# RWKV input stage of a two-layer transformer block: slab order, place of the convolution taps, convolution in four groups inside a slab, inverse begun inside the last input slab

## What is computed

```python
p = rms_norm(x, gain) @ w_in_first          # 2816 columns: 11 slabs of 256
# columns 0..1023: conformer convolution, the rest: RWKV inputs
h = u[..., :512] * sigmoid(u[..., 512:1024])        # "value" and "gate"
h = depthwise_conv(h, conv_w, 31 taps) + conv_b     # then layer_norm, silu
p = p + mu * (prev_token(p) - p)                     # token shift mix
r, k, v, w_lo, a_lo, g_lo = split(p)
w = exp(-exp(-0.5) * sigmoid(w0 + tanh(w_lo) @ w_up))
a = sigmoid(a0 + a_lo @ a_up);  g = sigmoid(g_lo) @ g_up
kk = normalise_per_head(k * k_k);  k = k * (1 + (a - 1) * k_a)
y = recurrence(r, w, k, v, kk, a)                    # S_t = S w - (S kk)(kk a) + v k
bonus = sum(r * k * r_k) * v
```

## Time and profile before

| | |
|---|---|
| median of 3 runs | 914.25 us |
| the profiled execution's own time | 913.55 us |
| its span, first to last instruction | 911.7 us |
| mean granted TensorE clock | 0.990 of full speed |
| TensorE matmul busy | 858.5 us (94%) |
| VectorE busy | 567.5 us (62%) |
| ScalarE busy | 440.0 us (48%) |
| chain that ended last: TensorE / VectorE / ScalarE | 79% / 12% / 4% |
| input stage, first slab's matmul to the level-1 `t_mm` products | 426.06 to 527.62 us |

### The profile page before, as it was taken

One profiled execution on the slowest core, in us unless ns is written; L12 is line 12 of the kernel. 1 busy time (PEld: TensorE's weight loads), 2 busy tenths in 40 slices (PEclk: granted clock), 3 DMA queues, 4 the chain that ended last, 5 costly groups with the idle time before them and its releaser, 6 DMA issues.

```text
span 911.7 us, 18606 instructions
## 1 busy us (share of the span) xinstructions
PE 858.5 (94%) x7952; PEld 797.7 (87%) x7952; DVE 567.5 (62%) x671; ACT 440.0 (48%) x558; POOL 20.8 (2%) x31
## 2 busy tenths in 40 slices
PE   4999999998999999998988989999899799999997
PEld 4899999987999998888986889888897799999885
DVE  4475467476777776647599886566554655555444
ACT  4555755445555556436472401445544544444333
POOL 1110000000000002000000000000000000000000
PEclk9999999999999999999999999999999799999999
DMA  9853433556455555455433121144524355555541
GB/s 346 287 183 115 173 139 139 186 208 220 160 176 180 184 179 191 179 185 202 168 125 110 48 96 50 48 155 160 171 95 141 112 185 184 184 184 184 185 139 46
DMA packets 22253, 145.86 MB, mean 160 GB/s; under 512 B 2618, under 2 KB 2810, under 8 KB 6064
## 3 DMA queue, kind: packets, MB, share of 16 engines
q1 hardware_dynamic: 19008, 134.23, 42.2%
q0 software_dynamic: 2896, 10.13, 3.4%
q10 hardware_dynamic: 288, 0.59, 0.2%
HBM read 143.87 MB, written 1.07 MB: 159 GB/s over the span
## 4 chain that ended last, share of the span: by engine, by line
PE 79%; DVE 12%; ACT 4%; issue 3%; DMA 1%; DVEq 0%; ACTq 0%
PE ps L1629 23%; PE ps L1631 22%; PE ps L1630 22%; DVE w_lo L935 4%; ACT w_hi L470 2%; PE ps L2025 2%; PE ps L1973 1%; PE ps L1657 1%; DVE cacc L1293 1%; DMA norm_gain<-in_rows_vec 1%; DVE xn L1525 1%; PE ps L2190 1%; PE ps L2206 1%; DVE xn L989 1%; DVE x L1531 1%
## 5 line engine op out<-in xcount | busy, mean ns | idle before, releaser
L935 DVE TENSOR_TENSOR w_lo<-raw,w_hi 128x2048 fp32r<-128x2048 f32 x124 | 284.8, 2297 | 189.2 <-ACT w_hi L470 189.2
L1629 PE MATMUL ps<-hT_hi,w_hi 128*128 128x256 f32 x1240 | 356.2, 287 | 13.2 <-DVE hT_lo L996 7.1
L1630 PE MATMUL ps<-hT_lo,w_hi 128*128 128x256 f32 x1240 | 352.9, 285 | 0.0
L1631 PE MATMUL ps<-hT_hi,w_lo 128*128 128x256 f32 x1240 | 352.9, 285 | 0.0
L470 ACT ACTIVATE w_hi<-raw 128x2048 fp32r<-128x2048 f32 x125 | 239.1, 1912 | 174.6 <-PE ps L1631 174.1
L1629 PEld LDWEIGHTS ps<-hT_hi,w_hi 128*128 128x128 f32 x1240 | 240.2, 194 | 19.0 <-issue 16.1
L1630 PEld LDWEIGHTS ps<-hT_lo,w_hi 128*128 128x128 f32 x1240 | 240.1, 194 | 0.1
L1631 PEld LDWEIGHTS ps<-hT_hi,w_lo 128*128 128x128 f32 x1240 | 240.1, 194 | 0.0
L1629 PE MATMUL ps<-w_hi,gT_hi 128*128 128x512 f32 x176 | 69.8, 397 | 0.6 <-DVE w_lo L935 0.6
L1631 PE MATMUL ps<-w_hi,gT_lo 128*128 128x512 f32 x176 | 69.0, 392 | 0.0
L1630 PE MATMUL ps<-w_lo,gT_hi 128*128 128x512 f32 x176 | 68.4, 388 | 0.0
(11 more groups left out here) (286 smaller groups left out, 1043.2 us busy)
## 6 DMA issues: line engine op xcount, KB each, us to landing
raw<-in_weights SPq DMA_DIRECT2D x126, 1024.0 KB, 4.9
row_gain<-in_rows_vec POOLq DMA_DIRECT2D x4, 512.0 KB, 4.8
norm_gain<-in_rows_vec POOLq DMA_DIRECT2D x4, 512.0 KB, 4.7
bias<-bias_scratch POOLq DMA_DIRECT2D x1, 1536.0 KB, 9.5
x<-in_x SPq DMA_DIRECT2D x2, 512.0 KB, 5.2
xn<-in_mem POOLq DMA_DIRECT2D x2, 512.0 KB, 5.8
out<-x SPq DMA_DIRECT2D x4, 256.0 KB, 2.1
masks<-in_masks POOLq DMA_DIRECT2D x1, 768.0 KB, 12.4
```

The costliest lines, as they stand in the source:

```text
L935: V.tensor_tensor(w_lo[:, n % SPLIT, :], raw[:, n % RAW, :], w_hi[:, n % SPLIT, :].bitcast(F32), ALU.subtract).then_inc(sems["lo_ready"], 1)
L1629: mm(dst, left[0], right[0], start=first, stop=False)
L1630: mm(dst, left[0], right[1], start=False, stop=False)
L1631: return mm(dst, left[1], right[0], start=False, stop=last)
```

## The change

It does five things, all in the stage `in2` and the levels behind it.

1. The order of the input slabs: gate half 1, value half 1, lora, k, k, gate half 0, value half 0, r, r, v, v. The lora products move from behind slab 2 to behind slab 4, and their first eight, of 64 rows each, are issued alternately from the two halves of the array's rows. `spread` does the same with four products of 64 rows in place of 128.
2. In each turn of the loop ScalarE and VectorE do `splits(n0+i+2)` first and the token shift or gate after it; VectorE's taps now stand ahead of that split (`TAPS_FIRST`), some behind (`TAPS_AFTER`), three inside turn 7.
3. The product k * k_k moves from VectorE to ScalarE (4 instructions, signal `kk_ready`). The product r * k * r_k is split: ScalarE scales k (4 instructions, `k_weighted`), VectorE multiplies by r in one instruction, in level 2; r * P goes to level 2 too. `feat_ready` no longer waits for r.
4. TensorE does the convolution as four groups of 64, 60, 64 and 60 products inside slab 8, one behind each fourth step, and `spread` behind step 7.
5. `pair_products(0)` stands ahead of slab 10, the turned products behind its step 5, the products with the identity behind its step 9.

Nothing is changed in SyncE's and GpSimd's lists; SyncE loads the same 11 slabs, of which three stand in another order.

```diff
-IN2 = {"lora": 0, "gate": (5, 1), "value": (6, 2), "k": (3, 4), "r": (7, 8), "v": (9, 10)}
+IN2 = {"lora": 2, "gate": (5, 0), "value": (6, 1), "k": (3, 4), "r": (7, 8), "v": (9, 10)}
...
             for i in range(11):
+                if i < 10:
+                    splits(n0 + i + 2)
                 if i in IN2["gate"]:
...
-                splits(n0 + i + 2)
-                if i == 1:
-                    wait_unit(u0)
+                if i == 3:
+                    wait_unit(u0 + IN2["lora"])
...
                 elif i == 5:
-                    act.wait_ge(sems["kk_ready"], 1)
+                    wait_unit(u0 + IN2["k"][1])
+                    for t in range(4):
+                        A(rt("kk", t), rt("k", t), ACT.Copy, scale=vec[:, VEC["k_k"] + t:VEC["k_k"] + t + 1])\
+                            .then_inc(sems["kk_ready"], 1)
+                    act.wait_ge(sems["kk_ready"], 4)
...
-                elif i == 7:
+                elif i == 8:
                     conv_out()
-                elif i == 8:
+                    act.wait_ge(sems["feat_ready"], 1)
+                    for t in range(4):
+                        A(rt("k", t), rt("k", t), ACT.Copy, scale=vec[:, VEC["r_k"] + t:VEC["r_k"] + t + 1])                            .then_inc(sems["k_weighted"], 1)
+                elif i == 9:
                     conv_total()
+            splits(n0 + 12)
...
-            TAP_PLAN = {2: 4, 3: 5, 4: 2, 5: 5, 6: 6, 7: 8, 8: 1}
+            TAPS_FIRST = {2: 2, 3: 2, 4: 3, 5: 3, 6: 2, 7: 2, 8: 2}
+            TAPS_AFTER = {1: 2, 7: 5, 8: 5}
             mixed = [0]
             for i in range(11):
+                conv_taps(TAPS_FIRST.get(i, 0))
+                if i == 7:
+                    dve.wait_ge(sems["kkrs_ready"], 1)
+                    V.reciprocal(rs[:, :], rs[:, :]).then_inc(sems["kkinv_ready"], 1)
+                splits(min(n0 + i + 2, FIRST_SLAB["mem_b"] - 1))
...
+                    settle()
+                    do(V.tensor_tensor(rwide("Pinv"), rwide("k"), rwide("Pinv"), ALU.mult))
+                    conv_taps(3)
                     dve.wait_ge(sems["kkb_ready"], 2)
...
+                if level == 2:
+                    dve.wait_ge(sems["feat_ready"], 1)
+                    wait_unit(u0 + IN2["r"][1])
+                    dve.wait_ge(sems["k_weighted"], 4)
+                    settle()
+                    V.tensor_tensor(rwide("Pprev"), rwide("k"), rwide("r"), ALU.mult).then_inc(sems["rk_ready"], 1)
+                    dve.wait_ge(sems["rk_ready"], 1)
+                    V.tensor_tensor(rwide("r"), rwide("r"), rwide("P"), ALU.mult).then_inc(sems["r_scaled"], 1)
...
-                for i, (rows, j) in enumerate(((slice(0, 64), 0), (slice(64, 128), 0), (slice(0, 128), 1))):
-                    for t in range(4):
...
+                for t in range(4):
+                    last = [product(i, slice(64 * i, 64 * i + 64), 0, t) for i in range(2)]
...
-                for t in range(4):
-                    last = mm(banks(b, 2)[:, t * T:(t + 1) * T], m("spread")[:, t * P:(t + 1) * P], rs[:, :],
+                for t in (0, 2, 1, 3):
+                    rows = slice(64 * (t // 2), 64 * (t // 2) + 64)
+                    last = mm(banks(b, 2)[:, t * T:(t + 1) * T], m("spread")[rows, t * P:(t + 1) * P], rs[rows, :],
...
+                if i == IN2["r"][1]:
+                    conv = convolution()
+                    for step, _ in enumerate(features_in_steps(n0 + i, u0 + i)):
+                        if step % 4 == 3:
+                            for _ in range(4):
+                                next(conv)
+                        if step == 7:
+                            pe.wait_ge(sems["kkinv_ready"], 1)
+                            spread(2, "kkb_ready")
+                elif i == 10:
+                    pe.wait_ge(sems["feat_ready"], 1)
+                    pair_products(0)
+                    for step, _ in enumerate(features_in_steps(n0 + i, u0 + i)):
+                        if step == 5:
+                            turned_products()
+                        elif step == 9:
+                            pe.wait_ge(sems["prod1_evac"], 1)
+                            blockwise(2, LT, lambda rows, u: m("ident_st")[rows, :], 0, 0, "l_mm")
+                else:
+                    used(features(n0 + i, u0 + i, None))
+                if i == 4:
+                    loras()
...
-            to_tokens(6, "k")
-            pe.wait_ge(sems["prod1_evac"], 1)
-            blockwise(2, LT, lambda rows, u: m("ident_st")[rows, :], 0, 0, "l_mm")
+            to_tokens(6, "Pinv")
...
-        kv[:MEM_A], in2[[10, 3, 1, 6, 7, 2, 0, 4, 5, 8, 9]], kv[MEM_A:MEM_A + MEM_B], rows(v["w_out_2"][0]),
+        kv[:MEM_A], in2[[3, 1, 10, 6, 7, 2, 0, 4, 5, 8, 9]], kv[MEM_A:MEM_A + MEM_B], rows(v["w_out_2"][0]),
```

More of the change, by code:

```diff
@@ L1319, in _ @@
                     mix_shifted(i)
[L1320 to L1327 removed]
+                if i == 1:
+                    wait_unit(u0 + i)
+                elif i == 4:
                     dve.wait_ge(sems["logw_ready"], 4)
@@ L1646, in features, with features_in_steps @@
                 return last
+            def features_in_steps(n, u):
+                bank_free(u)
+                hi, lo = slab(n)
+                for c in range(2):
+                    for k in range(KD):
+                        w = slice(k * T + c * P, k * T + (c + 1) * P)
+                        last = three(ps[:, u % 2, c * T:(c + 1) * T], (hi[:, w], lo[:, w]),
+                                     (hT_hi[:, k, :], hT_lo[:, k, :]), k == 0, k == KD - 1)
+                        if c == 1 and k == KD - 1:
+                            used(last)
+                        yield
             def unit_done(instruction):
@@ L1958, in to_tokens, with convolution @@
                 last.then_inc(sems["tok_ready"], 1)
-            def convolve():
+            def convolution():
                 pe.wait_ge(sems["taps_ready"], PE_TILES)
@@ L1975, in convolve @@
                                           stop=(r == TAPS_PER_GROUP - 1 or tap == TAPS - 1))
-                last.then_inc(sems["conv_mm"], 1)
+                        if t == PE_TILES - 1 and r == TAPS_PER_GROUP - 1:
+                            last.then_inc(sems["conv_mm"], 1)
+                        yield
             def conv_totals():
@@ L2031, in stacked, with turned_products @@
                 return lambda rows, u: a[rows, u, :]
+            def turned_products():
+                pe.wait_ge(sems["cacc_ready"], PE_TILES)
+                for t in range(4):
+                    for mt in range(TT):
+                        for half in range(2):
+                            cols, at = slice((2 * mt + half) * CHUNK, (2 * mt + half + 1) * CHUNK), (2 * t + mt) * CHUNK
+                            last = mm(ps[chunk_rows(half + 1), 4, at:at + CHUNK], rt("beta", t)[64:128, cols],
+                                      rt("kk", t)[64:128, cols], start=True, stop=True)
+                last.then_inc(sems["turned_ready"], 1)
             def conv_moment(u, src):
@@ L2038, in conv_moment @@
                 unit_done(last)
+            n0, u0 = FIRST_SLAB["in2"], FIRST_UNIT["in2"]
+            pe.wait_ge(sems["late_in"], 16)
+            for i in range(11):
+                if i == 0:
+                    operand(FILL["g0"], KD - 1)
+                if i == IN2["r"][1]:
[20 more added lines that the diff above has]
+                    loras()
+                elif i == 6:
+                    pe.wait_ge(sems["kksq_ready"], 1)
+                    head_rows(3, "r", "kksum_ready")
+                elif i == 9:
+                    conv_totals()
             def memory_groups():
```

82 lines of the change are left out of this document (19 added, 63 removed).

## The result

| | before | after |
|---|---|---|
| median of the runs | 914.98 us (4 runs, 914.17 to 915.99) | 903.49 us (4 runs, 902.60 to 904.10) |
| profiled execution | 913.55 us, span 911.7 | 904.10 us, span 902.3 |

The ratio of the medians is 0.9873, 95% interval 0.9856 to 0.9890: faster by 11.5 us. The forecast was 904.2, a gain of 10.0 at the products `t_mm`. The two profiled executions lie 9.4 apart. The median gains 2 us more than the trace can account for; the last experiments look for those. The forecast's base was the median of three runs, 914.25; beside the change, with a fourth run, it is 914.98.

A forecast was written before the change was run, and what follows sets the result against it. The input stage was taken as TensorE's own work plus stalls, mostly of VectorE's making. With 13.7 us gone and new costs added, `t_mm` came 10.0 earlier: 913.55 - 10.0 = 903.55, plus 0.7 for the median, 904.2 us; range 901.5 to 909.0.

The forecast's parts named there:

- `t_mm` within 0.1 of its bounds: Sign in the profile after: the level-1 products `t_mm` start at 517 to 518 us, before at 527.62.
- the wait for `prod1_evac`: Sign at the products with the identity: TensorE waits 1 to 2 us, released by VectorE's mask.
- The waits for `w_lo` and `glu` go, 5.0: Input stage: TensorE's waits for VectorE's split and `glu` vanish because the split comes first and `glu` earlier, 5.0 us less.
- The fetch stalls, 3.5 down to 0.5: Convolution: three TensorE instruction-fetch stalls costing 3.5 us shrink to one partial stall of 0.5 (bounds 0 and 3.5).
- The inverse's waits, 1.9 and 1.0: Start of the inverse: TensorE's two waits, for VectorE's L1392 and a PSUM bank, go, saving 1.9 and 1.0 us.
- Loras 1.5 and `spread` 0.8: Products alternating between row halves overlap fully: loras 1.5 us less (bounds 0 and 1.5), `spread` 0.8 less (0 to 0.8).
- Switching, 0.2 per round trip: Slabs 8 and 10: changing between whole-array and tiled matmuls costs 0.2 us per round trip, 1.0 in all.
- The new wait of 1.7 for VectorE's mask: Products with the identity, slab 10: TensorE arrives at 506.7, VectorE's mask ends at 508.2, TensorE goes on at 508.4.
- The end: Behind the identity products: `t_mm` at 517.6, 10.0 us earlier; level 2 costs 0 (bounds 0 and 1.0), output projection 0.
- VectorE is later: Rival: VectorE's 50 us without pause run 8% longer, TensorE waits 4 us; gain 6, 908.2 us, chance 0.15.
- The stalls stay: Rival: the convolution's three issue stalls remain wherever the products stand; gain 8.7, 905.5 us, chance 0.1.
- Slower, by the switches: Rival: retiling in slabs 8 to 10 drops TensorE's clock to half speed; 7.6 us slower, 921.9, chance 0.04.

The follow-up runs named there:

- the last experiments: The kernel before, unchanged, profiled twice more to look at its granted clock: 913.95 and 917.66 us.
- the fuller try: The change with ScalarE's token copies and an output-projection rounding moved earlier, a VectorE split and the convolution's centring moved later: 904.14 us, ratio 0.9885.

## Why the prediction was right

The median, 903.49, is 0.7 from the forecast. That is partly luck: the gain in the trace was 9.4 to 9.5, not 10.0, and 2 us of the gain in the medians are not from the stage at all. Of the signs named beforehand, these came: no wait for `w_lo`, at most one stall, `t_mm` within 0.1 of its bounds. The loras in 3.0 us and the wait for `prod1_evac` did not. Step by step:

- **The waits for `w_lo` and `glu` go, 5.0.** They went. The reason was wrong. I put it down to the split standing first; with the split last they stay away, and with the split first alone the kernel before gets slower by 5.2. What is left of the change as their cause is its other parts: the order of the slabs, which gives `glu` a slab's lead, the new places of the taps, and the work that left this half of VectorE's turn. These were not tried apart, so the cause of the largest term stays open.
- **The fetch stalls, 3.5 down to 0.5.** Right. The group at 488.31 takes 3.26, the others 2.62 to 2.69, so one stall of 0.6 is left, at TensorE's pass 3767, where one had been before. In other runs with the four groups the same group takes 2.69 to 3.67, so this stall is anything from 0 to 1.0. The mechanism is shown by the 64 passes put in and by the packets. What I missed is that the groups also bring VectorE its columns in time: in one piece the stage lost 5.0.
- **The inverse's waits, 1.9 and 1.0.** Both gone from their places, the second back as the 0.9 for the k tokens, forecast at 0.8. Beginning inside the slab was worth 1.8 up to the transposes of v.
- **Loras 1.5 and `spread` 0.8.** The loras gave 0.97 of 1.5: pairs on the two row halves overlap only in part. `spread` gave 0.75 against the kernel before, from 1.82 to 1.07, and 0.6 against the run with the pairs undone.
- **Switching, 0.2 per round trip.** Too low in the convolution. From 478.69 to 495.82 are 17.13 us; `spread` takes 1.07 and 36 passes of the slab, at 0.122, 4.40. The 11.66 left stand against my 10.7: 9.6 of convolution, 0.5 of stall and 0.6 of switches. If the convolution proper still costs 9.6, a round trip costs 0.5 and not 0.2. Most of this is in the groups: the three without a stall take 0.0216 per pass, against 0.0195.
- **The new wait of 1.7 for VectorE's mask.** It did not come. VectorE ended the mask at 508.45, against 508.2 forecast, so the sum of 50.7 us over some seventy instructions was out by 0.25. Its start was right as well (457.49 against 457.5); VectorE then idled 0.9 where 0.5 was allowed. TensorE was 2.2 late, at 508.9 against 506.7: about 0.6 of loras and `spread`, 1.0 of convolution, 0.1 of slab 0's start and 0.5 in small pieces behind the convolution. It walked into the time that it would have waited.
- **The end.** Behind that place my 508.4 became 508.91, and the 0.5 was carried to `t_mm`: 518.07 against 517.6. The forecast is not quite one sum: its terms (13.7 gone; 1.0, 0.5, 1.7 and 0.8 new) make 9.7, its walk along the timeline 10.0. The 0.3 lies between level 1's start and `t_mm`, where the walk has 2.8 us and the trace 3.05. Level 2 cost nothing (its wait 1.33 from start to start, 1.53 before). At the output projection `spread` saved TensorE time and the wait for `w_lo` took it back, 1.4 before and 2.1 now, and 1.4 again with the pairs undone.

At this one wait an error was covered: TensorE's work was sized 2.2 too small, but the 1.7 that it was to wait for VectorE, whose sum was right, took most of that up. Between two engines that meet, an error counts only by how far it makes the later one later, here 0.5 of 2.2.

Of the rivals, "VectorE is later" was not met, though the test shows how near it was: 2.6 us more of its work cost 2.2. "The stalls stay" fell by the four groups, which take all but one of them away, and the shifted passes show why. "Slower, by the switches" is not seen: no stretch at the lower level stood between 426 and 520 us in the change. In the kernel before with the split first one did, behind 4.4 us in which TensorE idled of 10.4.

**What stays open** is the 2 us between the medians' gain (11.5 to 12.0) and the traces' (9.4 to 9.5). The executions of the kernel before had a mean clock of 0.983 to 0.988 beside the first group of experiments, the eight of the change 0.988 to 0.990; and the three profiled executions put the difference outside the stage. A clock that is lower by 0.003 over 910 us is 2.7 us. Whether the change has a part in where the clock falls elsewhere, or which kernel's executions fall in luckier places, these runs don't tell. The kernels that are the change with one small edit had 0.985 to 0.987 (the split last), 0.982 to 0.989 (the fuller try) and 0.988 to 0.990 (the pairs undone), so some small edits lose the advantage again and others keep it.

## What to carry to other kernels

When two engines run neck and neck, sum both up to the place where they meet, and put the uncertainty on the later one; a test that adds work to one of them tells its slack in a single run, if what was added is measured in the trace and not taken from the plan (here 2.63 us in place of 2.4). A dense stream of small matmuls should be cut into pieces with full-size work between them, for the instruction fetch as for the engine that waits for that work. An edit that helps in a new order of work can harm in the old one, so the reason for a gain has to be tried by itself before it is carried anywhere.

## What was not expected of the hardware

- TensorE stalls for 0.9 to 1.35 us, start to start, at fixed counts of its own passes in a stream of 32x32 products: behind passes 3639, 3767 and 3895 of the program, 0.6 to 1.6 us over three executions of the kernel before, and up to 2.4 in the one with 64 passes put in. Each ends 1.2 to 1.4 us behind a 16 KB packet of the instruction queue in the traces of the two kernels. With twelve full passes behind every 120 or 128 small ones a single one, of 0.6, was left. The Trainium skill (Runtime: NRT & Kernel Launch, Instruction fetch mechanics) counts this fetch as hidden; the rows differ, and they decide.
- Twelve lora products, of which eight alternate between the two row halves, take 3.57 us; all in turn they take 4.54. Full overlap of the eight would have made it 3.0.
- In executions of one kernel, stretches at the 1.2 GHz level vary in length (3.4 or 6.8 us at 214 to 228 us) and in whether they come at all (at 56 us in one of three). Each of them costs about half its length (slab 0 stands 1.4 us later in the execution where the stretch ahead of it is 3.4 us longer and all else alike). That is up to 4 us between executions, with a stage in the middle that repeats within 0.2 us. Distances inside a trace tell more than the medians here.
